# Forgetting attention in an fp32 block kernel: sums of squares of Q and K beside the projection, inverse norms and forget rows spread through DRAM

## The reference, cut to what matters

```python
def fox_mixer(h, w_in, b_f, q_gain, k_gain, w_out):
    q, k, v, f_logit = jnp.split(h @ w_in, [hd, 2 * hd, 3 * hd], axis=-1)
    q = rms_norm_2(q.reshape(bsz, seq, N_HEADS, HEAD_DIM), q_gain)
    k = rms_norm_2(k.reshape(bsz, seq, N_HEADS, HEAD_DIM), k_gain)
    ...
    log_f = jax.nn.log_sigmoid(f_logit.astype(jnp.float32) + b_f.astype(jnp.float32))
    cum = jnp.cumsum(log_f, axis=1).transpose(0, 2, 1)
    ...
        s = jnp.einsum('bqhd,bshd->bhqs', qb, k, preferred_element_type=jnp.float32) * scale
        s = s + (cq[..., :, None] - cum[:, :, None, :])
        return _causal_softmax(s, start, v)
    return _sweep_query_blocks(block, seq) @ w_out
```

## Time and profile before

| | us |
|---|---|
| median of 3 runs | 2737.25 (2732.31 to 2739.13) |
| the profiled execution, its own time | 2738.28 |
| its span, first to last instruction | 2736.2 |
| PE busy | 2590.1 (95%) |
| DVE busy | 1494.1 (55%) |
| ACT busy | 1111.3 (41%) |
| mean granted TensorE clock | 0.976 |

### The profile page before, as it was taken

One profiled execution on the slowest core, in us unless ns is written; L12 is line 12 of the kernel. 1 busy time (PEld: TensorE's weight loads), 2 busy tenths in 40 slices (PEclk: granted clock), 3 DMA queues, 4 the chain that ended last, 5 costly groups with the idle time before them and its releaser, 6 DMA issues.

```text
span 2736.2 us, 57092 instructions
## 1 busy us (share of the span) xinstructions
PE 2590.1 (95%) x24185; PEld 2525.9 (92%) x24185; DVE 1494.1 (55%) x1681; ACT 1111.3 (41%) x1051; POOL 69.2 (3%) x69
## 2 busy tenths in 40 slices
PE   6999979788999999999999799998989999999999
PEld 6999878487989999999999799977989999999999
DVE  5457556475455454444444544547467667666444
ACT  3334423332344445453333433344345555554333
POOL 1000130000100000000010000000100000000000
PEclk8999999789999999999999899999999999999999
DMA  5555200001545555555555355530545555556654
GB/s 166 195 189 197 79 3 4 1 1 63 177 149 196 188 196 189 194 191 193 194 184 167 108 192 194 189 123 17 184 154 197 186 199 185 199 186 197 190 195 154
DMA packets 169214, 421.74 MB, mean 154 GB/s; under 512 B 17462, under 2 KB 22139, under 8 KB 168859
## 3 DMA queue, kind: packets, MB, share of 16 engines
q1 hardware_dynamic: 168699, 419.13, 45.8%
q10 hardware_dynamic: 416, 1.18, 0.1%
HBM read 418.16 MB, written 2.10 MB: 154 GB/s over the span
## 4 chain that ended last, share of the span: by engine, by line
PE 88%; DVE 9%; ACT 2%; issue 1%; SPq 0%; DMA 0%; DVEq 0%; POOL 0%; ACTq 0%; POOLq 0%
PE ps L1596 26%; PE ps L1597 26%; PE ps L1598 26%; DVE LOW L891 1%; PE ps L1636 1%; DVE NSQ L925 1%; ACT HIW L519 1%; PE ps L1721 1%; PE ps L1731 1%; PE ps L1693 1%; PE ps L1750 1%; PE ps L1686 1%; PE ps L1728 1%; PE ps L2017 1%; PE ps L1985 1%
## 5 line engine op out<-in xcount | busy, mean ns | idle before, releaser
L891 DVE TENSOR_TENSOR LOW<-RAW,HIW 128x2048 fp32r<-128x2048 f32 (+2 forms) x400 | 909.9, 2275 | 1021.9 <-ACT HIW L519 1021.7
L1596 PE MATMUL ps<-H_ROWS,HIW 128*128 128x256 f32 x4928 | 1372.7, 279 | 43.5 <-DVE LOW L891 21.5
L1597 PE MATMUL ps<-H_ROWS,HIW 128*128 128x256 f32 x4928 | 1371.1, 278 | 0.0
L1598 PE MATMUL ps<-H_ROWS,LOW 128*128 128x256 f32 x4928 | 1370.0, 278 | 0.0
L519 ACT ACTIVATE HIW<-RAW 128x2048 fp32r<-128x2048 f32 (+2 forms) x400 | 761.0, 1903 | 1203.1 <-PE ps L1598 1202.1
L1596 PEld LDWEIGHTS ps<-H_ROWS,HIW 128*128 128x128 f32 x4928 | 932.6, 189 | 47.2 <-issue 25.8
L1598 PEld LDWEIGHTS ps<-H_ROWS,LOW 128*128 128x128 f32 x4928 | 933.4, 189 | 0.0
L1597 PEld LDWEIGHTS ps<-H_ROWS,HIW 128*128 128x128 f32 x4928 | 931.8, 189 | 0.0
L1596 PE MATMUL ps<-HID,HIW 128*128 (+1 forms) x1408 | 390.4, 277 | 1.3 <-DVE LOW L891 1.3
L1598 PE MATMUL ps<-HID,LOW 128*128 (+1 forms) x1408 | 390.3, 277 | 0.0
L1597 PE MATMUL ps<-HID,HIW 128*128 (+1 forms) x1408 | 390.3, 277 | 0.0
(11 more groups left out here) (354 smaller groups left out, 1715.9 us busy)
## 6 DMA issues: line engine op xcount, KB each, us to landing
RAW<-in_ffn_w_up SPq DMA_DIRECT2D x264, 512.0 KB, 4.3
RAW<-in_ffn_w_down SPq DMA_DIRECT2D x176, 512.0 KB, 4.6
RAW<-in_w_in SPq DMA_DIRECT2D x96, 512.0 KB, 4.1
RAW<-in_fox_w_in SPq DMA_DIRECT2D x96, 512.0 KB, 4.3
RAW<-in_ffn_w_gate SPq DMA_DIRECT2D x88, 512.0 KB, 3.6
RAW<-in_w_out SPq DMA_DIRECT2D x32, 512.0 KB, 4.9
RAW<-in_fox_w_out SPq DMA_DIRECT2D x32, 512.0 KB, 5.0
RAW<-in_w_in SPq DMA_DIRECT2D x4, 576.0 KB, 4.8
```

Of the source, the lines that this page charges most:

```text
L891: V.tensor_tensor(LOW[:, u_const % 4, 0:n], RAW[:, u_const % 4, 0:n], HIW[:, u_const % 2, 0:n].bitcast(F32), ALU.subtract).then_inc(lo_mad ...
L1596: mm(o_, hi_w, h_hi, start=start, stop=False)
L1597: mm(o_, hi_w, h_lo, start=False, stop=False)
L1598: i = mm(o_, lo_w, h_hi, start=False, stop=stop)
```

## The change

Beside groups 1 to 4 of the projection the squares of the group before (8 heads of Q or K) are made by ScalarE (SQF), split to a high and a low part (SQH, SQL), and summed by 16 fp32r matmuls that TensorE does in the last unit of the group, into the unused half of bank 0 (`sum_squares`). VectorE reads them at the evacuation (`evac_and_variance`), ScalarE takes the root and VectorE the reciprocal in the next group; the row goes to a DRAM tensor rows_out and is read back once for each partition (INV), and VectorE scales the eight heads in units 6 and 7. The forget gates are worked on beside group 0; their rows go to DRAM and back to all partitions in group 1 (CB), and VectorE adds the causal mask in groups 2 and 3 (CB, CB0). The forget sum of the query is no longer added to the scores. In the heads one `tensor_tensor_reduce` makes the negated biased scores and their minimum. The values are turned to tokens inside the first eight heads, four transposes by TensorE to bank 7 and a copy by VectorE each. The projection's loops are written out on all three engines. The second unit's halves for U_OUT2 are made after the heads. `forget(j)` holds the old lines L1439 to L1459 without the first memset; `constants()` waits for the causal mask and copies the one-hot columns to sel1r. Of the prologue's removed lines the diff leaves most out: they are L824 to L836, L1463 to L1491 and L1980 to L2021 of the kernel before.

```diff
-        ASQ = at("ASQ", [P, 32, T], r2 + 50176)
-        CB = at("CB", [P, A_HEADS, 3, P], r2 + 66560)
+        SQF = at("SQF", [P, 8, T], r2 + 50176)
+        SQH = at("SQH", [P, 8, T], r2 + 58368, F32R)
+        SQL = at("SQL", [P, 8, T], r2 + 32768, F32R)
+        INV = at("INV", [P, 8, T], r2 + 40960)
+        CB = at("CB", [P, A_HEADS, T], r2 + 66560)
+        CB0 = at("CB0", [P, A_HEADS, P], r2 + 82944)
+        sel1r = at("sel1r", [P, 32], masks + 512, F32R)
...
-            group_phase(U_FOX, 4)
-
-            for g in (4, 5):
-                for j in range(2, UG + 2):
+            for g in range(6):
+                for j in range(2, UG + 2 if g < 5 else UG + 1):
                     hi(U_FOX + g * UG + j)
-                    if (g, j) == (4, 3):
+                    if (g, j) == (0, 3):
                         got("softplus_abs")
                         A(FW[f_in, 1, :], FW[f_in, 1, :], ACT.Exp, scale=-1.0).then_inc(S("softplus_exp"), 1)
-                    if (g, j) == (4, 5):
+                    if (g, j) == (0, 5):
                         got("softplus_plus1")
                         A(FW[f_in, 1, :], FW[f_in, 1, :], ACT.Ln).then_inc(S("softplus_ln"), 1)
...
+                    if (g, j) == (1, 4):
+                        act.wait_ge(S("forget_summed"), 1)
+                        act.dma_start(rows_out[0:16, :], FW[112:128, 2, :]).then_inc(S("row_kept"), 16)
+                    if (g, j) == (1, 5):
+                        act.wait_ge(S("row_kept"), 16)
+                        act.dma_start(CB[:], rows_out[0:16, :].unsqueeze(0).broadcast_to([P, A_HEADS, T]))\
+                            .then_inc(S("forget_rows"), 16)
+                    if g >= 2 and j == 2:
+                        act.wait_ge(S("ss_rows"), 2 * g - 3)
+                        A(FW[0:16, 0, :], FW[0:16, 0, :], ACT.Sqrt).then_inc(S("ss_root"), 1)
+                    if 1 <= g <= 4 and j == 2:
+                        act.wait_ge(bank_freed, N_FOX + 8 * g + FREE_BANKS)
+                        if g > 1:
+                            act.wait_ge(S("sq_lo"), g - 1)
+                        A(SQF[:], QKV[:, 8 * g - 8:8 * g, :], ACT.Square).then_inc(S("sq_split"), 1)
+                    if 1 <= g <= 4 and j == 3:
+                        if g > 1:
+                            act.wait_ge(S("ss_summed"), g - 1)
+                        act.wait_ge(S("sq_split"), 2 * g - 1)
+                        A(SQH[:], SQF[:], ACT.Copy).then_inc(S("sq_split"), 1)
+                    if g >= 2 and j == 3:
+                        act.wait_ge(S("ss_rows"), 2 * g - 2)
+                        act.dma_start(rows_out[8 * g:8 * g + 8, :], FW[0:8, 0, :]).then_inc(S("row_kept"), 16)
+                    if g >= 2 and j == 4:
+                        act.wait_ge(S("row_kept"), 16 * g)
+                        if g > 2:
+                            act.wait_ge(S("qk_normed"), 8 * (g - 2))
+                        act.dma_start(INV[:], rows_out[8 * g:8 * g + 8, :].unsqueeze(0).broadcast_to([P, 8, T]))\
+                            .then_inc(S("inv_rows"), 16)
+
+
             for h in range(A_HEADS + 2):
                 z = h % 2
                 if h < A_HEADS:
+                    got("score_max", 2)
                     for n, c0, w in ((0, 0, P), (1, P, T)):
-                        got("score_max")
-                        A(SC[:, h % 3, c0:c0 + w], SC[:, h % 3, c0:c0 + w], ACT.Exp, bias=AST[:, h % 3, n:n + 1],
-                          accum_out=AST[:, h % 3, 2 + n:3 + n]).then_inc(S("prob_made"), 1)
+                        A(SC[:, h % 3, c0:c0 + w], SC[:, h % 3, c0:c0 + w], ACT.Exp, scale=-1.0,
+                          bias=AST[:, h % 3, n:n + 1], accum_out=AST[:, h % 3, 2 + n:3 + n]).then_inc(S("prob_made"), 1)
                 if 0 < h <= A_HEADS:
                     got("pt_turned")
                     A(PT[:, 1 - z, :], ps[3 - z][:, 0:384], ACT.Copy).then_inc(S("pt_made"), 1)
                 if h > 1:
                     got("att_summed")
                     A(H(0, h - 2, h - 1)[:, 0, :], ps[4 + z][:, 0:T], ACT.Copy).then_inc(S("att_hi"), 1)
+            hi(U_OUT2 + 1)
...
-            group_phase(U_FOX, 4, evac_fox)
...
+            def scale_heads(octet, some):
+                dve.wait_ge(S("inv_rows"), 16 * (octet + 1))
+                c = COL["fox_q_gain_2" if octet < 2 else "fox_k_gain_2"]
+                for i in some:
+                    s1 = QKV[:, 8 * octet + i, :]
+                    V.scalar_tensor_tensor(s1, s1, vec[:, c:c + 1], INV[:, i, :], ALU.mult, ALU.mult)\
+                        .then_inc(S("qk_normed"), 1)
+
+            def masked(dst, src):
+                dve.wait_ge(S("forget_rows"), 16)
+                V.tensor_tensor(dst, src, causal[:].unsqueeze(1).broadcast_to([P, A_HEADS, P]), ALU.add)\
+                    .then_inc(S("bias_made"), 1)
+
+            def evac_and_variance(g):
+
+                summed(M_FOX, 0, U_FOX + UG, g)
+                V.tensor_copy(QKV[:, g * 8, :], ps[0][:, 0:T])
+                dve.wait_ge(S("ss_summed"), g)
+                a, e = (1.0, P * 1e-6) if g <= 2 else (1.0 / P, 1e-6)
+                ins = V.tensor_scalar(FW[0:16, 0, :], ps[0][0:16, T:2 * T], a, e, ALU.mult, ALU.add)
+                ins.then_inc(S("ss_rows"), 1)
+                dve.wait_ge(S("ss_rows"), 2 * g - 1)
+                dve.sem_inc(bank_freed, 1)
+                for f in range(1, GROUP):
+                    summed(M_FOX, f, U_FOX + UG, g)
+                    V.tensor_copy(QKV[:, g * 8 + f, :], ps[f][:, 0:T]).then_inc(bank_freed, 1)
+
+            for g in range(6):
+                for j in range(2, UG + 2 if g < 5 else UG + 1):
                     lo(U_FOX + g * UG + j)
...
-            def biased(h):
...
+                    elif j == UG:
+                        evac_and_variance(g)
+                    if g == 0:
+                        forget(j)
+                    if 1 <= g <= 4 and j == 4:
+                        dve.wait_ge(S("sq_split"), 2 * g)
+                        V.tensor_tensor(SQL[:], SQF[:], SQH[:].bitcast(F32), ALU.subtract).then_inc(S("sq_lo"), 1)
+                    if g >= 2 and j == 2:
+                        dve.wait_ge(S("ss_root"), g - 1)
+                        V.reciprocal(FW[0:16, 0, :], FW[0:16, 0, :]).then_inc(S("ss_rows"), 1)
+                    if (g, j) == (2, 5):
+                        masked(CB[:, :, P:T], CB[:, :, P:T])
+                    if (g, j) == (3, 5):
+                        masked(CB0[:], CB[:, :, 0:P])
+                    if g >= 2 and j in (6, 7):
+                        scale_heads(g - 2, range(0, 4) if j == 6 else range(4, 8))
+            dve.wait_ge(S("bias_made"), 2)
+
+            def negative_scores(h):
                 z = h % 3
                 got("scores_made")
                 if h > 2:
                     got("pt_turned")
-                for n, c0, w, blk in ((0, 0, P, 0), (1, P, T, 1)):
-                    src = CB[:, h, blk:blk + w // P, :].rearrange("p b t -> p (b t)")
-                    step(V.scalar_tensor_tensor(SC[:, z, c0:c0 + w], src, FQ[:, n, h:h + 1], ps[SCORE_BANKS[z]][:, c0:c0 + w],
-                                                ALU.subtract, ALU.add))
-                settle()
-                for n, c0, w in ((0, 0, P), (1, P, T)):
-                    V.tensor_reduce(AST[:, z, n:n + 1], SC[:, z, c0:c0 + w], AX_X, ALU.max, negate=True)\
-                        .then_inc(S("score_max"), 1)
+                for n, c0, w, bias in ((0, 0, P, CB0), (1, P, T, CB)):
+                    V.tensor_tensor_reduce(SC[:, z, c0:c0 + w], ps[SCORE_BANKS[z]][:, c0:c0 + w], bias[:, h, :],
+                                           -1.0, 3e38, ALU.add, ALU.min, AST[:, z, n:n + 1]).then_inc(S("score_max"), 1)
+
+            def value_copy(i):
+                got("turned_v")
+                V.tensor_copy(VT[:, i % 2, (i // 2) * 512:(i // 2 + 1) * 512], ps[7][:, :]).then_inc(S("vt_made"), 1)
 
             def normalised(h):
                 z = h % 3
@@ -1520,13 +1557,16 @@
                     .then_inc(S("att_made"), 1)
             for h in range(A_HEADS + 3):
                 if h < A_HEADS:
-                    biased(h)
+                    negative_scores(h)
+                if h < 8:
+                    value_copy(h)
                 if 0 < h <= A_HEADS:
                     normalised(h - 1)
                 if h > 2:
                     out_lo(h - 3)
 
 
+            lo(U_OUT2 + 1)
...
+                    if beside is not None and kk == len(tiles) - 1:
+                        beside()
...
-            group_phase(U_FOX, N_FOX, 6)
-
-
...
+
+            def sum_squares(g):
+                pe.wait_ge(S("sq_lo"), g)
+                if g > 1:
+                    pe.wait_ge(S("ss_rows"), 2 * g - 3)
+                for i in range(8):
+                    pick = sel1r[:, 15 - i:31 - i]
+                    mm(ps[0][0:16, T:2 * T], pick, SQH[:, i, :], start=False, stop=False, skip_group_check=True)
```

(83 more changed lines are left out.)

86 lines of the change are left out of this document (4 added, 82 removed).

## The result

| | before | after |
|---|---|---|
| median, beside each other on one chip | 2737.77 us (2732.31 to 2739.13, 4 runs) | 2699.43 us (2695.15 to 2702.69, 4 runs) |
| the profiled execution, its own time | 2738.28 | 2702.69 |
| its span | 2736.2 | 2701.0 |
| group 0's unit 2 to the last high half | 1559.41 to 1810.48: 251.07 | 1559.65 to 1819.51: 259.86 |
| end of last evacuation to last half of H_ROWS | 1817.37 to 1902.05: 84.68 | 1826.40 to 1869.84: 43.44 |

The ratio is 0.9868, 95% interval 0.9855 to 0.988: 1.3% faster, 38 us where 30 were forecast (2707.6). In the two profiled executions the two stretches of the table that the change touches give -41.24 and +8.79, so -32.5 us; the span is 35.2 us shorter.

What follows compares the result with a forecast made beforehand. TensorE was taken to bound the projection and VectorE the head loop. Heads 38.9 us less, matmuls 7.3 more: 31.6 saved; 2738.28 - 31.6 + 2.0 = 2708.7, or 2707.6 for the median (chance 0.50), range 2697 to 2722.

Steps and rivals of the forecast that it cites:

- The main term: From last evacuation to output projection: sums, tables and reciprocal leave the path, 46.1 us against 84.99, 38.9 less.
- The sums: TensorE in groups 1 to 4: 64 added matmuls at the stream's 0.1135 us each cost 7.3 us.
- upper end: Highest price for the 64 added matmuls: the old sums' 0.218 us a record, so 14.0 us.
- The ring: First eight heads: value copy, scaling, turn, mix, scores and transposes wait on each other, 3.68 us a head against 2.28.
- drain: Behind the last head's scaling, up to the output projection: 3.89 us, as in the kernel before.
- A: Rival: early heads go at VectorE's own 2.55 us and the combined operation costs 0.73: 2698 us; chance 0.15.
- Late heads: Heads behind the first eight: 1.95 us each, nine of them 17.55, with the combined pair at 0.93.
- the 1.6 us: Late heads, if ScalarE's 0.19 us record counts in full for both operations: 2.13 us each, nine 1.6 more.
- The clock: Head loop: one early head's turn at half clock, 1.2 GHz, adds 2.0 us.
- B: Rival: half clock through the first heads' whole stage, 14.4 us instead of 2.0: 2720 us; chance 0.22.
- The stream's cover: Beside the projection: added ScalarE, VectorE and transfer work fits waiting time plus 1.2 us, cost 0; stores have 3.5 us.
- C: Rival: the stream falls behind as ScalarE waits for a DRAM row; 2742 us at 15 us a store; chance 0.13.

Runs made afterwards that it cites:

- e5: The kernel before, profiled once more with no edit: heads 83.35 us against 84.68, span 2729.9 us against 2736.2.
- e3: Changed kernel with the squares' high half alone summed, 8 matmuls a group in place of 16: median 2692.83 us, ratio 0.9855 to the kernel before.
- e2: Changed kernel with VectorE scaling head h-1 before it copies V of head h, nothing left out: median 2686.95 us, ratio 0.9838 to the kernel before.
- e4: Changed kernel with the combined operation undone into scalar_tensor_tensor and then tensor_reduce: median 2702.4 us, ratio 0.9897 to the kernel before.
- e7: Changed kernel with ScalarE's Square made three times in unit 2 of groups 1 to 4: median 2708.72 us, ratio 0.9918 to the kernel before.
- e1: The changed kernel run again with no edit (also e1_changed): median 2694.13 us, ratio 0.9868 to the kernel before.
- e6: Changed kernel with the 2 MB spread of forget rows issued twice: median 2705.9 us, ratio 0.9909 to the kernel before.

## Why the prediction was right, step by step

**The main term, right.** The sums, the tables and their reciprocal left the path, and the heads became late next: 84.68 to 43.44, -41.2 us against a forecast of -38.9 (or -36.9 with the clock's 2.0). Of this 1.3 is luck of the first profile, whose heads had the fall of the clock (e5); against e5 it is -39.9.

**The sums, right.** 258.48 - 251.07 = 7.41 us for 64 (forecast 7.3; upper end 14.0). e3 shows 3.72 for half. The upper end was the price of a record of f32 matmuls, and the new ones are fp32r; their 16-column weights cost no more than full ones.

**The ring, right and shown.** 3.75 us a head against 3.68; scaling of head 1 at 6.07 us after the evacuation (6.26), head 6 at 24.82 (24.66), drain 3.87 (3.89). e2 removes it by order alone: A is out, for the early heads.

**Late heads, too dear.** They took 1.68 us on average instead of 1.95, and nine of them 2.5 us less than forecast. The term was the combined pair at 0.93. Measured, its two operations start 0.20 and 0.34 us before what follows, 0.54 in all, below the 0.73 that the prediction held for the floor. The 0.73 was the length of the present pair, which reads a third operand. From start to start that pair takes 0.76, the pair of e4 without the third operand 0.65, and the combined pair 0.54. Whether the third operand or the order of the operands costs the first 0.11 was not tried. In the sum the new pair stood for 0.76 + 0.20 = 0.96; of the 0.42 that it took less, 0.15 came back as idle time of VectorE, and 0.27 a head is left. A's 0.73 was nearer, and still too dear. The Trainium skill (VectorE: DVE Perf Modes, Two Vector instructions with no wait between them) says such an operation is two instructions: the trace agrees, with a second record of 0.08 us. But the next instruction starts together with that record, so it takes no time of its own, and the 1.6 us that the prediction worked out from ScalarE's records did not come.

**The clock, wrong.** The 2.0 us taken for one ring at 1.2 GHz did not come; B needed seven of them. With 61% to 64% busy in the ring, the granted clock stayed at 1.00, and in none of the eight profiled executions of changed kernels did it fall in the heads. The row that the term rested on was chance: the kernel before fell to 0.50 in the fill of the loop in its first profile and not in its second, with the same instructions ahead of it. So it is not shown that the change took away a cause. Why the one execution fell stays open.

**The stream's cover, right, and a part of it closer than thought.** Square, Copy, Sqrt and table load cost nothing; e7 shows what they would cost without the cover. No row in DRAM was waited for: C is out. The time free for it was 5.0 us and not 3.5: the store was issued at 1656.17, before the Copy had started, and the spread at 1661.15. No run records when a stored row landed. The Trainium skill (DMA: Bandwidth & Descriptors, Anatomy of one DMA) gives the fixed 2 us, by which the prediction held that wait for safe, for transfers that GpSimd issues; ScalarE issues these. But the transfers were priced only by when they land themselves. What they do to the weights stood in no term: the 2 MB spread made one weight unit late by 0.7 us of the 1.2 free, and twice that traffic cost 7.3 us, 4.6 as a stop of TensorE and the rest at the lower clock behind it.

**The sum.** Of the profiled execution 2708.7 was forecast and 2702.7 came, 6.0 us less. Heads 4.3 less (clock 2.0, late heads 2.5, while ring and fill took 0.2 more); stream 1.5 more, since group 0 ran at the slow pace; behind the heads 3.0 less, of which 11 x 0.21 = 2.3 since the output projection ran at the fast pace throughout and 11 of before's units at the slow one. The paces are chance, and so these two are luck, good and bad. The rest is 0.2 at the start and the 0.4 by which time and span differ.

**Open.** The medians give a gain of 37.5 and 38.3 us, e1's stretches 258.48 - 251.07 - 41.2 = -33.8, or 1.3 less without the fall of the clock. The tail (831 to 834 us) and the start of the stream (1551 to 1560) differ between executions of all kernels by more than the 4 to 6 us that are missing. Whether the change makes the other stretches a little shorter or the sample did is not settled.

## What to carry to other kernels

Where two engines take turns through in-order queues, write the ring down, from one instruction back to itself, and ask of each step whether the next head needs it: one copy placed ahead of a scaling cost 8.65 us here, and moving it was free. Price an operation by the time to the next start in a row with the same operands: the old pair, with an operand that the new one does not have, was no floor (0.73 against 0.54). A clock seen in one execution is one sample: profile the kernel before twice. And a transfer beside a weight stream needs two prices: when it lands, and how late it makes the weights.

## What the runs showed of the hardware

- TensorE has two paces at the same granted clock of 1.00: a 256-column matmul every 0.113 or 0.118 us, units of 5.44 or 5.65 us, by whole stretches and by chance. In the ten executions between 0 and 38 of about 390 units were slow. A pace held from one stop or group boundary to a later one, and the same stretches came up slow again: the first six units of the output projection in four of the ten. This alone moves the span by up to 38 x 0.21 = 8 us.
- VectorE's add, minimum and statistic in one operation, from PSUM: records of 0.28 us for 128 columns and 0.42 for 256, starts 0.20 and 0.34 before the next; the separate operations in e4 take 0.62 + 0.61 for the pair, 0.65 + 0.53 from start to start.
- A spread of 2 MB from a 16 KB row in DRAM landed in 8.8 us beside the weights, one of 1 MB in 7.2 us. While the 2 MB one is under way (e1_changed, busy time by stretch) the DMA share is 0.98:
```profile
1615.00:1620.00 5.00, 5.00 (x46) 5.00 (x46) 1.85 (x2) 1.92 (x1) 0.00 (x0) 1.00 0.98 406
```
- In e6 the granted clock was 1.00 until TensorE had stopped for 4.6 us, and then 0.50: the stream's matmuls went 0.21 us apart instead of 0.113. In the fill of the old head loop it fell in one of two executions of the same program, for 1.3 us of time.
